# The prompt tile's scan step moved into the last stages of the make stage

## The chip, the cores and the metric

The kernel runs on one core of a Trainium2 chip. The metric is the time of one execution in device microseconds (us). TensorE (PE in the profile) does the matmuls and transposes, VectorE (DVE) and ScalarE (ACT) the element work on PSUM and SBUF, GpSimd (POOL) element work on SBUF alone, and SyncE (SP) issues most DMAs. Each engine runs its own program in order and waits on semaphores.

## The reference, cut to what matters

One layer of a diffusion backbone runs on 128 prompt tokens and 512 sample tokens: a feed-forward block, a mixer, a second feed-forward block. The mixer has two halves, attention and a gated delta rule that scans over the tokens in both directions:

```python
sol = lax.linalg.triangular_solve(a_mat, rhs, left_side=True, lower=True, unit_diagonal=True)
u0, w = sol[..., :dv], sol[..., dv:]
def step(state, inp):
    qg_n, kg_n, u0_n, w_n, qk_n, gl_n = inp
    u = u0_n - jnp.einsum('bhcd,bhde->bhce', w_n, state)
    o = jnp.einsum('bhcd,bhde->bhce', qg_n, state) + jnp.einsum('bhcs,bhse->bhce', qk_n, u)
    state = state * gl_n[..., None, None] + jnp.einsum('bhcd,bhce->bhde', kg_n, u)
    return state, o
...
y = jnp.concatenate([o_a.reshape(...), o_b_att.reshape(...)], axis=-1) @ lp['w_out']
```

The prompt starts from a zero state and its last state is an output (`new_state_delta`). The sample starts from a state that is an input (`state_delta`). So the scan of the prompt gives nothing to the scan of the sample.

## The kernel before

The 640 tokens lie in five tiles of 128 (`NT = 5`); tile 0 is the prompt. After attention the mixer goes through three parts.

**The make stage** builds, for each tile and each half of the heads, a decayed and inverted matrix (`t_all`) and a decayed product of q and k (`p_all`). There are ten units of work. Each is a sequence of 26 stages, a new unit starts every 7 stages (`MAKE_STAGES, MAKE_LAG = 26, 7`), and unit u uses the buffers and the two PSUM banks of chain u % 4. `make_schedule()` yields the pieces stage by stage, and every engine walks the same list. Units 6 and 7, the last ones of the third and fourth chain, end in stages 67 and 74; stages 75 to 88 hold only units 8 and 9, on the first and second chain. Within a unit each level of the inversion is a round trip: TensorE multiplies (L2148, L2152) or transposes (L2155), VectorE masks or subtracts the result (L1449, L1454, L1458), TensorE goes on. GpSimd masks the other operand (L1653).

**The scan** has five steps s = 0 to 4; step 0 is the prompt tile. Each step has four blocks b (two directions, two halves of the heads), each in its own PSUM bank 4 + b:

- `scan_a` (L2168; not in step 0): products of k and q with the state. VectorE makes the right side r from it (`scan_r`, L1464 and L1467: the second one reads two SBUF tensors), ScalarE scales the q part (L903).
- `scan_b` (L2184): times the inverted matrix; VectorE scales the result to u (`scan_u`, L1473).
- `scan_c` (L2194, L2198): update of the state and the output of the block; VectorE or ScalarE adds or copies them (L1483, L1495, L893).

GpSimd cuts the matrices of a step to a triangle (L1662 for `scan_b`, L1673 for `scan_c`), eight instructions a step, into `t_one` and `p_one`, which are the make buffers of the first and second chain.

**The output projection of the attention half** is cut into 16 pieces, `attention_part(0..15)`, each of 12 matmuls with 320 columns (L1683 to L1685). They are put between the stages of the scan to fill TensorE. Four pieces use one weight tile, which ScalarE rounds (`w_high`, L547) and VectorE subtracts (`w_low`, L995, two SBUF inputs); after each two pieces VectorE adds a block to x (`update_attention`, L1046). The weight slots `w_hi` and `w_lo` 0 and 1 lie on the same SBUF bytes as the make buffers of the third and fourth chain (`spare` in the profile). So before, the two first weight tiles were split after the whole make stage, beside scan step 0. Behind the scan come the normalization and gate of the scan's output (L1515, L1523, L1530 on VectorE), four transposes a tile (L2247), and then the other half of the output projection, which waits for the last of them.

In what order pieces and stages stand on TensorE is written by hand:

```python
            for s in range(NT):
                for stage in (scan_a, scan_b, scan_c):
                    if s == 0 and stage is scan_a:
                        continue
                    for b in range(4):
                        stage(s, b)
                    if (s, stage) != (0, scan_b):
                        attention_part(next(parts))
```

Before, piece 0 follows `scan_c` of step 0, pieces 1 to 12 follow the stages of steps 1 to 4, and 13 to 15 lie between the transposes.

## Time and profile before

| | us |
|---|---|
| median of 3 runs | 1739.75 |
| lowest and highest run | 1727.72, 1741.33 |
| the profiled execution | 1740.31 |
| its span in the trace | 1738.5 |
| TensorE busy in the span | 1648.7 (95%) |
| VectorE, ScalarE, GpSimd busy | 948.7, 512.9, 202.1 |
| mean granted TensorE clock | 0.97 of full speed |

The profiled execution lies 1.8 us over its own span and 0.6 us over the median. The three runs are 13.6 us apart, 0.8% of the time. TensorE is the engine that matters nearly everywhere, so the reading goes by what makes it wait and by the clock that it is granted.

### The profile page before, as it was taken

What the parts mean: (1) busy time and instruction counts of PE and PEld (TensorE: products, weight loads), DVE (VectorE), ACT (ScalarE), POOL (GpSimd) and SP (SyncE); (2) the same over time, 40 slices, a digit from 0 to 9 for tenths busy, and PEclk for the clock granted to TensorE, in tenths of its full rate; (3) what the DMA queues carried; (4) which work ended last, traced back from release to release, by engine and by line L of the source; (5) the groups of instructions that cost most, each with busy time, mean ns of one, the idle gap of its engine ahead of it and who ended that gap; (6) DMA issues with size and microseconds to landing.
All of it is one profiled execution on the core that took longest, in us unless ns stands there. A gap on an engine that the chain in (4) does not pass through costs nothing.

```text
span 1738.5 us, 27319 instructions
## 1 busy us (share of the span) xinstructions
PE 1648.7 (95%) x10807; PEld 1547.8 (89%) x10807; DVE 948.7 (55%) x1770; ACT 512.9 (30%) x978; POOL 202.1 (12%) x165
## 2 busy tenths in 40 slices
PE   6899999999999999999978999799799999999998
PEld 4899999999999999966667888799799999998886
DVE  5866666775456574447647788448652322222233
ACT  4522222221224334424441110154342222222223
POOL 0000000000000000110026666545000000000000
PEclk9999999999999999997789999899899999999999
DMA  9444444444343222210000000011212222222222
GB/s 279 124 134 142 136 144 143 137 135 141 99 144 110 56 75 64 61 49 1 1 7 1 1 1 1 1 32 37 85 37 73 72 72 75 81 61 88 71 82 88
DMA packets 183811, 136.53 MB, mean 79 GB/s; under 512 B 8192, under 2 KB 169269, under 8 KB 183605
## 3 DMA queue, kind: packets, MB, share of 16 engines
q1 hardware_dynamic: 161029, 112.91, 21.8%
q10 hardware_dynamic: 22704, 22.55, 4.3%
q8 instruction: 53, 0.87, 0.2%
q14 instruction: 25, 0.20, 0.0%
HBM read 132.03 MB, written 3.41 MB: 78 GB/s over the span
## 4 chain that ended last, share of the span: by engine, by line
PE 83%; DVE 9%; SPq 2%; issue 2%; ACT 2%; DMA 1%; POOL 0%; DVEq 0%; ACTq 0%; POOLq 0%
PE ps L1683 19%; PE ps L1685 18%; PE ps L1684 18%; PE ps L2148 3%; PE ps L1830 3%; PE ps L1828 3%; PE ps L1829 3%; PE ps L2152 3%; PE ps L2036 2%; SPq L425 2%; PE ps L1739 1%; PE ps L2184 1%; PE ps L2198 1%; PE ps L2057 1%; DMA w_raw<-in_w_ffn_in 1%
## 5 line engine op out<-in xcount | busy, mean ns | idle before, releaser
L1683 PE MATMUL ps<-h_hi,w_lo 128*128 128x320 f32 x1760 | 554.3, 315 | 12.5 <-DVE h_lo L1530 6.4
L1685 PE MATMUL ps<-h_hi,w_hi 128*128 128x320 f32 x1760 | 547.2, 311 | 0.0
L1684 PE MATMUL ps<-h_lo,w_hi 128*128 128x320 f32 x1760 | 547.0, 311 | 0.0
L995 DVE TENSOR_TENSOR w_lo<-w_raw,w_hi 128x1024 fp32r<-128x1024 f32 x158 | 195.8, 1241 | 377.4 <-ACT w_hi L547 376.2
L1683 PEld LDWEIGHTS ps<-h_hi,w_lo 128*128 128x128 f32 x1760 | 333.6, 190 | 17.0 <-DVE h_lo L1530 6.7
L1684 PEld LDWEIGHTS ps<-h_lo,w_hi 128*128 128x128 f32 x1760 | 333.5, 190 | 1.1 <-issue 0.7
L1685 PEld LDWEIGHTS ps<-h_hi,w_hi 128*128 128x128 f32 x1760 | 333.3, 189 | 0.0
L547 ACT CAST w_hi<-w_raw 128x1024 fp32r<-128x1024 f32 x158 | 165.1, 1047 | 261.6 <-PE ps L1685 111.4
L1127 DVE SCALAR_TENSOR_TENSOR ada_acc<-ada_ffn,cond,ada_acc 128x256 f32<-128x256 f32 x336 | 139.0, 480 | 1.1
L641 ACT CAST act_hi<-scratch 128x640 f32 (+1 forms) x44 | 32.0, 727 | 292.0 <-DVE scratch L1167 292.0
L1683 PE MATMUL ps<-act_hi,w_lo 128*128 128x320 f32 (+1 forms) x352 | 109.5, 311 | 0.0
L1684 PE MATMUL ps<-act_lo,w_hi 128*128 128x320 f32 (+1 forms) x352 | 108.7, 309 | 0.0
L1685 PE MATMUL ps<-act_hi,w_hi 128*128 128x320 f32 (+1 forms) x352 | 108.7, 309 | 0.0
L1828 PE MATMUL ps<-w_hi,act_lo 128*128 128x512 f32 x220 | 87.1, 396 | 1.0 <-DVE w_lo L995 1.0
L1830 PE MATMUL ps<-w_hi,act_hi 128*128 128x512 f32 x220 | 87.5, 398 | 0.0
L1829 PE MATMUL ps<-w_lo,act_hi 128*128 128x512 f32 x220 | 86.8, 394 | 0.0
L1167 DVE TENSOR_TENSOR scratch<-square,ps 128x640 f32<-128x640 f32 x44 | 36.1, 820 | 87.9 <-PE ps L1685 87.9
L634 ACT ACTIVATE square<-ps 128x640 f32<-128x640 f32 x44 | 31.0, 705 | 171.4 <-PE ps L1685 171.1
L1683 PEld LDWEIGHTS ps<-act_hi,w_lo 128*128 128x128 f32 x352 | 66.2, 188 | 0.1
L1684 PEld LDWEIGHTS ps<-act_lo,w_hi 128*128 128x128 f32 x352 | 66.2, 188 | 0.1
L1685 PEld LDWEIGHTS ps<-act_hi,w_hi 128*128 128x128 f32 x352 | 66.2, 188 | 0.0
L1618 POOL MEMSET pre<- 128x24 f32 x3 | 0.2, 122 | 547.3 <-PE ps L1685 547.3
(299 smaller groups left out, 2500.6 us busy)
## 6 DMA issues: line engine op xcount, KB each, us to landing
w_raw<-in_w_ffn_in SPq DMA_DIRECT2D x88, 512.0 KB, 3.9
w_raw<-in_w_ffn_out SPq DMA_DIRECT2D x44, 512.0 KB, 3.7
ada_ffn<-in_w_ada ACTq DMA_DIRECT2D x43, 512.0 KB, 4.2
w_raw<-in_w_in SPq DMA_DIRECT2D x28, 512.0 KB, 3.8
ada_ffn<-in_w_ada SPq DMA_DIRECT2D x13, 512.0 KB, 4.8
ada_tile<-in_w_ada SPq DMA_DIRECT2D x10, 512.0 KB, 8.6
w_raw<-in_w_out SPq DMA_DIRECT2D x8, 512.0 KB, 3.5
ada_wide<-in_w_ada SPq DMA_DIRECT2D x3, 1024.0 KB, 9.5
```

What stands on the lines that cost most here:

```text
L547: nc.scalar.copy(w_hi[s if slot is None else slot], w_raw[s][:]).then_inc(w_hi_ready, 1)
L995: nc.vector.tensor_tensor(w_lo[at], w_raw[s][:], w_hi[at].bitcast(F32), ALU.subtract)\
L1127: ins = nc.vector.scalar_tensor_tensor(a, w, col, a, op0=ALU.mult, op1=ALU.add)
L1167: nc.vector.tensor_tensor(halves(act_f[par][:]), halves(silu_g[par][:]), ps[:, 4 * par + 2:4 * par + 4, 0:HT], ALU.mult).then_inc(act_read ...
L1683: nc.tensor.matmul(out, lo, xh, start=start, stop=False)
L1684: nc.tensor.matmul(out, hi, xl, start=False, stop=False)
L1685: return nc.tensor.matmul(out, hi, xh, start=False, stop=stop)
L1828: nc.tensor.matmul(out, lo, wh, start=first, stop=False)
L1829: nc.tensor.matmul(out, hi, wl, start=False, stop=False)
L1830: ins = nc.tensor.matmul(out, hi, wh, start=False, stop=last)
L2148: four(c, lambda out, h: nc.tensor.matmul(out, m_t[c][:, h, :], t_cols[c][:, h, :], start=True, stop=True))
L2152: four(c, lambda out, h: nc.tensor.matmul(out, x_w[c][:, h, :], tt_cols[c][:, h, :], start=True, stop=True))
```

## The change

The masks, `scan_b`, `scan_u` and `scan_c` of step 0 are called from inside the walk over the make stage. `make_schedule()` yields an extra mark at the head of each stage, and at marks 69 to 81 the engines take the pieces of step 0. The masks go into the third and fourth chain's buffers (`t_first`, `p_first`), which are free from stages 68 and 75 on. ScalarE splits the first two weight tiles after step 0, and VectorE's `w_low` of the first stands now behind `scan_r` of step 1, ahead of piece 0. The pieces are dealt anew: 0 to 8 after the stages of steps 1 to 3, none after `scan_a` of step 4, 9 after its `scan_b`, and 10 to 15 behind the last `scan_c`. VectorE's `w_low` of the third and fourth weight tile moves from the middle of steps 2 and 3 to their ends; on ScalarE `w_high` goes ahead of the next step's `scan_kg` (the scaling of k, L883).

```diff
@@ constants @@
+TWO_DONE = 6 * MAKE_LAG + MAKE_STAGES
+THREE_DONE = TWO_DONE + MAKE_LAG
@@ buffers, make_schedule @@
+            t_first, p_first = [x[0] for x in spare], [x[1] for x in spare]
             for at in range((2 * NT - 1) * MAKE_LAG + MAKE_STAGES):
+                yield None, at, 0, 0, 0
@@ ScalarE @@
-            for c in range(4):
-                act.wait_ge(t_pe[c], ROUNDS[c] * PE_T)
-            for m in range(2):
-                w_high(TILE_WOUT + m, m)
...
+            for b in range(4):
+                scan_first(b)
+            for b in range(4):
+                scan_kg(1, b)
+            for m in range(2):
+                w_high(TILE_WOUT + m, m)
@@ VectorE, inside and behind the make stage @@
+                if k is None:
+                    if c == THREE_DONE + 1:
+                        scan_u(0, 0)
+                        scan_u(0, 1)
+                    if c == THREE_DONE + 2:
+                        scan_u(0, 2)
+                        scan_u(0, 3)
+                    continue
...
+            for b in range(2, 4):
+                scan_out(0, b)
+            for s in range(1, NT):
+                for b in range(4):
+                    scan_r(s, b)
+                if s == 1:
+                    w_low(TILE_WOUT, 0)
                 if s == NT - 1:
-                    update_attention(4)
                     for p in range(OUT_EARLY):
                         o_mean(p)
                 for b in range(4):
                     scan_u(s, b)
-                if s == 0:
-                    w_low(TILE_WOUT, 0)
+                if s == 1:
                     w_low(TILE_WOUT + 1, 1)
-                if s == 1:
-                    update_attention(0)
                 if s == 2:
-                    w_low(TILE_WOUT + 2, 0)
-                if s == 3:
-                    update_attention(3)
-                    w_low(TILE_WOUT + 3, 1)
+                    update_attention(1)
                 for b in range(4):
-                    if 1 <= s < NT - 1:
+                    if s < NT - 1:
                         scan_state(s, b)
-                    if s >= 1 or b >= 2:
-                        scan_out(s, b)
-                if s in (1, 2):
-                    update_attention(s)
+                    scan_out(s, b)
+                if s < NT - 1:
+                    update_attention((0, 2, 3)[s - 1])
+                if s in (2, 3):
+                    w_low(TILE_WOUT + s, s % 2)
@@ GpSimd, inside the make stage @@
+                if k is None:
+                    if c == TWO_DONE + 1:
+                        pool.wait_ge(t_dve[2], ROUNDS[2] * DVE_T)
+                    if c == THREE_DONE:
+                        pool.wait_ge(t_dve[3], ROUNDS[3] * DVE_T)
+                    if TWO_DONE < c <= TWO_DONE + 4:
+                        mask_t(0, c - TWO_DONE - 1)
+                    if THREE_DONE <= c < THREE_DONE + 4:
+                        mask_p(0, c - THREE_DONE)
+                    continue
@@ TensorE, inside the make stage and in the scan @@
+                if k is None:
+                    if c == THREE_DONE:
+                        scan_b(0, 0)
+                        scan_b(0, 1)
+                    if c == THREE_DONE + 1:
+                        scan_b(0, 2)
+                        scan_b(0, 3)
+                    if THREE_DONE + 3 <= c < THREE_DONE + 7:
+                        scan_c(0, c - THREE_DONE - 3)
+                    continue
...
-            for s in range(NT):
+            for s in range(1, NT):
                 for stage in (scan_a, scan_b, scan_c):
-                    if s == 0 and stage is scan_a:
-                        continue
                     for b in range(4):
                         stage(s, b)
-                    if (s, stage) != (0, scan_b):
+                    if (s, stage) != (NT - 1, scan_a):
                         attention_part(next(parts))
+            attention_part(next(parts))
```

Before, on TensorE, the end of the make stage and the head of step 0 (chain 0's and 1's matmuls on `m_t`, `t_cols`, `x_w`, `tt_cols`; `m_t0` to `x_w1` in the L2184 rows hold the triangle-cut matrices, `v_tok` is v, `r_s` holds u):

```order
L2152 MATMUL ps<-tt_cols1,x_w1 128x128 x4
L2155 MATMUL ps<-ident,t_all 128x128 x4
L2148 MATMUL ps<-t_cols1,m_t1 128x128 x4
L2152 MATMUL ps<-tt_cols1,x_w1 128x128 x4
L2184 MATMUL ps<-v_tok,m_t0 128x64 x4
L2184 MATMUL ps<-v_tok,m_t1 128x64 x4
L2184 MATMUL ps<-v_tok,x_w0 128x64 x4
L2184 MATMUL ps<-v_tok,x_w1 128x64 x4
L2194 MATMUL ps<-r_s0,square0 128x128 x2
L2198 MATMUL ps<-r_s0,t_cols0 128x64 x4
```

After, on TensorE, stages 76 to 80 (`spare20` and `spare30` are two of the masked matrices in the third chain's buffers, `spare01` one in the fourth chain's; L2175 is `scan_b`, L2185 and L2189 are `scan_c`, L2233, L2237 and L2240 the make stage's old L2148, L2152 and L2155):

```order
L2233 MATMUL ps<-t_cols1,m_t1 128x128 x4
L2175 MATMUL ps<-v_tok,spare20 128x64 x4
L2175 MATMUL ps<-v_tok,spare30 128x64 x4
L2240 MATMUL ps<-ident,t_all 128x128 x4
L2237 MATMUL ps<-tt_cols1,x_w1 128x128 x4
L2233 MATMUL ps<-t_cols0,m_t0 128x128 x4
L2240 MATMUL ps<-ident,t_all 128x128 x4
L2185 MATMUL ps<-r_s0,square0 128x128 x2
L2189 MATMUL ps<-r_s0,spare01 128x64 x4
L2237 MATMUL ps<-tt_cols0,x_w0 128x128 x4
```

Step 0 no longer follows the make stage but stands between the pieces of its last two units, while both are still in work.

Before, on VectorE, from the last instruction of the make stage into step 1 (`pre` is where the scan's output lies, `egc` the decay):

```order
L1454 TENSOR_TENSOR t_all<-t_all,ps 128x512
L1473 TENSOR_TENSOR r_s0<-ps,beta 128x256
L1473 TENSOR_TENSOR r_s1<-ps,beta 128x256
L1473 TENSOR_TENSOR r_s2<-ps,beta 128x256
L1473 TENSOR_TENSOR r_s3<-ps,beta 128x256
L995 TENSOR_TENSOR w_lo0<-w_raw0,w_hi0 128x1024
L995 TENSOR_TENSOR w_lo1<-w_raw1,w_hi1 128x1024
L1495 TENSOR_TENSOR pre<-pre,ps 128x256 x2
L1464 TENSOR_TENSOR r_s0<-ps,egc 128x256
```

After, on VectorE, the same place:

```order
L1502 TENSOR_TENSOR t_all<-t_all,ps 128x512
L1461 TENSOR_TENSOR pre<-pre,ps 128x256 x2
L1430 TENSOR_TENSOR r_s0<-ps,egc 128x256
L1433 TENSOR_TENSOR r_s0<-v_tok,r_s0 128x256
L1430 TENSOR_TENSOR r_s1<-ps,egc 128x256
L1433 TENSOR_TENSOR r_s1<-v_tok,r_s1 128x256
L1430 TENSOR_TENSOR r_s2<-ps,egc 128x256
L1433 TENSOR_TENSOR r_s2<-v_tok,r_s2 128x256
L1430 TENSOR_TENSOR r_s3<-ps,egc 128x256
L1433 TENSOR_TENSOR r_s3<-v_tok,r_s3 128x256
L998 TENSOR_TENSOR w_lo0<-w_raw0,w_hi0 128x1024
```

The split of the first weight tile, which piece 0 waits for, stood ahead of all of step 1 and stands now behind the eight instructions of its `scan_r`.

## Rows read from the trace of the kernel before

**Rows 1.** Windows: stretch, length, busy PE PEld DVE ACT POOL (instructions), clock, DMA

```profile
1087.30:1101.50 14.20, 12.40 (x96) 10.75 (x94) 9.32 (x15) 0.00 (x0) 5.09 (x4) 1.00 0.00 1
1101.50:1112.10 10.60, 5.95 (x40) 4.71 (x40) 4.13 (x6) 0.00 (x0) 2.52 (x2) 1.00 0.00 0
1112.10:1134.95 22.85, 20.60 (x94) 20.63 (x95) 7.46 (x9) 11.37 (x40) 21.67 (x16) 0.55 0.03 7
1134.95:1205.23 70.28, 67.79 (x565) 67.53 (x564) 43.28 (x107) 36.77 (x138) 37.51 (x32) 1.00 0.11 33
1205.23:1221.40 16.17, 9.65 (x70) 9.13 (x69) 15.58 (x29) 6.31 (x12) 0.00 (x0) 0.96 0.11 32
```

**Rows 2.** Chain of waits in the make stage's end: start, us, what

```profile
1077.59 0.89 PE ps L2148 x8
1078.48 0.44 PE ps L2144 x4
...
1088.20 0.70 DVE x_w L1449
1088.94 1.16 PE ps L2152 x8
1090.10 0.91 PE ps L2148 x8
```

**Rows 3.** Chain of waits in step 0 (to 1134) and step 1

```profile
1114.35 7.05 PE ps L2184 x32
1121.40 0.96 PE ps L2194 x4
1122.36 1.60 PE ps L2198 x8
...
1134.95 3.58 PE ps L2168 x32
...
1140.29 3.52 PE ps L2184 x32
...
1146.90 0.50 PE ps L2194 x4
1147.40 0.84 PE ps L2198 x8
```

**Rows 4.** Windows of TensorE alone where the clock was low: busy (instructions), clock, DMA

```profile
1114.35:1131.40 17.05, 17.05 (x80) 0.50 0.00 1
1131.40:1134.85 3.45, 3.45 (x15) 0.50 0.16 38
1221.40:1227.05 5.65, 5.64 (x21) 0.50 0.31 93
```

**Rows 5.** Timeline, GpSimd's masks and VectorE's two-input instructions: start, us, instruction

```profile
1122.75 4.46 POOL L1662 TENSOR_TENSOR m_t<-t_all,cst 128x512 f32<-128x512 f32 x2
1121.78 4.31 DVE L995 TENSOR_TENSOR w_lo<-w_raw,w_hi 128x1024 fp32r<-128x1024 f32 x2
...
1212.31 1.22 DVE L995 TENSOR_TENSOR w_lo<-w_raw,w_hi 128x1024 fp32r<-128x1024 f32 x1
...
1178.32 0.42 DVE L1464 TENSOR_TENSOR r_s<-ps,egc 128x256 f32<-128x256 f32 x1
...
1179.65 1.04 DVE L1467 TENSOR_TENSOR r_s<-v_tok,r_s 128x256 f32<-128x256 f32 x1
```

**Rows 6.** Timeline, the end of step 2 and step 4 (in brackets: idle time, releaser)

```profile
1170.77 1.23 DVE L995 TENSOR_TENSOR w_lo<-w_raw,w_hi 128x1024 fp32r<-128x1024 f32 x1 [8.73 <-ACT w_hi L547]
1172.99 0.38 PE L2168 MATMUL ps<-st,pre 128*128 128x128 f32 x1 [2.49 <-DVE pre L1495]
...
1198.98 1.53 DVE L1473 TENSOR_TENSOR r_s<-ps,beta 128x256 f32<-128x256 f32 x4
```

**Rows 7.** Timeline, GpSimd's first free place from stage 68 on

```profile
1071.82 1.27 POOL L1653 TENSOR_TENSOR spare<-t_all,cst 128x512 f32<-128x512 f32 x1 [1.30 <-DVE t_all L1454]
```

**Rows 8.** Timeline, TensorE behind the scan and the normalization

```profile
1221.41 0.63 PE L1683 MATMUL ps<-h_hi,w_lo 128*128 128x320 f32 x1 [6.43 <-DVE h_lo L1530]
```

More of the change, by code:

```diff
@@ new lines, in scan_u, with scan_state @@
+            def scan_u(s, b):
+                d, g, t, q = where(s, b)
+                dve.wait_ge(c_pe[b], scan_at("pe", s, b, "b"))
+                nc.vector.tensor_tensor(heads4(u_s[b][:], DK), heads4(ps[:, 4 + b, 0:256], DK),
+                                        spread(beta[:, t, q:q + 4], DK), ALU.mult).then_inc(c_dve[b], 1)
+            def scan_state(s, b):
+                d, g, t, q = where(s, b)
+                dve.wait_ge(c_pe[b], scan_at("pe", s, b, "c"))
+                dve.wait_ge(c_act[b], scan_at("act", s, b, "dec"))
+                for e in range(2):
+                    rows, cols = slice(e * DK, e * DK + DK), slice(e * DK, e * DK + DK)
+                    S = st[1][rows, d, 2 * g:2 * g + 2, cols]
+                    ins = nc.vector.tensor_tensor(S, S, heads4(ps[rows, 4 + b, 0:256], P)[:, :, cols], ALU.add)
+                ins.then_inc(c_dve[b], 1)
@@ L2116, in four, with scan_a @@
                 ins.then_inc(t_pe[c], 1)
-            for k, c, r, t, g in make_schedule():
+            def scan_a(s, b):
+                d, g = b // 2, b % 2
+                t = tile_of(s, d)
+                if s == 1:
+                    pe.wait_ge(st_in, 64)
+                    pe.wait_ge(c_act[b], scan_at("act", 0, b, "o" if b < 2 else "S"))
+                if s >= 2 or b >= 2:
+                    pe.wait_ge(c_dve[b], scan_at("dve", s - 1, b, "o"))
+                for which, at in ((4, 0), (0, 256)):
+                    for cc in range(2):
+                        ins = nc.tensor.matmul(ps[:, 4 + b, at + cc * P:at + cc * P + P],
+                                               pre[:, which + 2 * g + cc, t * P:(t + 1) * P], st[1][:, d, 2 * g + cc, :],
+                                               start=True, stop=True)
+                ins.then_inc(c_pe[b], 1)
@@ new lines, in scan_b @@
+            def scan_b(s, b):
+                if s == 0:
+                    pe.wait_ge(t_dve[2 + b // 2], ROUNDS[2 + b // 2] * DVE_T)
+                else:
+                    pe.wait_ge(c_dve[b], scan_at("dve", s, b, "r"))
+                    pe.wait_ge(c_act[b], scan_at("act", s, b, "oq"))
+                pe.wait_ge(c_pool[b], scan_at("pool", s, b, "t"))
+                r = v_tok[:, tile_of(0, b // 2), (b % 2) * 256:(b % 2) * 256 + 256] if s == 0 else r_s[b][:]
+                for h in range(4):
+                    ins = nc.tensor.matmul(ps[:, 4 + b, h * DK:(h + 1) * DK], (t_one if s else t_first)[b][:, h, :],
+                                           r[:, h * DK:(h + 1) * DK], start=True, stop=True)
+                ins.then_inc(c_pe[b], 1)
@@ new lines, in scan_c @@
+            def scan_c(s, b):
+                pe.wait_ge(c_dve[b], scan_at("dve", s, b, "u"))
+                if s < NT - 1:
+                    pe.wait_ge(c_act[b], scan_at("act", s, b, "kg"))
+                    for cc in range(2):
+                        nc.tensor.matmul(ps[:, 4 + b, cc * P:(cc + 1) * P], kg[b][:, cc * P:(cc + 1) * P],
+                                         u_s[b][:, cc * P:(cc + 1) * P], start=True, stop=True)
+                pe.wait_ge(c_pool[b], scan_at("pool", s, b, "p"))
+                for h in range(4):
+                    ins = nc.tensor.matmul(ps[:, 4 + b, 256 + h * DK:256 + (h + 1) * DK], (p_one if s else p_first)[b][:, h, :],
+                                           u_s[b][:, h * DK:(h + 1) * DK], start=True, stop=True)
+                ins.then_inc(c_pe[b], 1)
@@ L2173, in scan_b @@
-            def scan_b(s, b):
-                if s == 0:
-                    for c in (2, 3):
-                        pe.wait_ge(t_dve[c], ROUNDS[c] * DVE_T)
-                else:
-                    pe.wait_ge(c_dve[b], scan_at("dve", s, b, "r"))
-                    pe.wait_ge(c_act[b], scan_at("act", s, b, "oq"))
-                pe.wait_ge(c_pool[b], scan_at("pool", s, b, "t"))
-                r = v_tok[:, tile_of(0, b // 2), (b % 2) * 256:(b % 2) * 256 + 256] if s == 0 else r_s[b][:]
-                for h in range(4):
-                    ins = nc.tensor.matmul(ps[:, 4 + b, h * DK:(h + 1) * DK], t_one[b][:, h, :],
-                                           r[:, h * DK:(h + 1) * DK], start=True, stop=True)
-                ins.then_inc(c_pe[b], 1)
```

151 lines of the change are left out of this document (57 added, 94 removed).

## Prediction

> **What bounds the kernel now.** The first view is the page: TensorE is busy for 95% of the span, so elsewhere the change could only shift waits. It touches 1070 to 1222 us, and there the windows are the view to start from [rows 1]. The reader is to see four different limits. Up to 1101.5 us two units are in work and TensorE is nearly full; from there to 1112.1 one unit is left and TensorE works 5.95 of 10.6 us. From 1112.1 to 1134.95 (step 0 and piece 0) it is full, but at a granted clock of 0.55. In steps 1 to 4 it is full at full clock, 67.8 of 70.3 us. In the last stretch it works 9.65 of 16.2 us and VectorE 15.6: there VectorE sets the end.
>
> The chain of waits then gives the price of each piece at both clocks [rows 3]. `scan_b` of four blocks is 7.05 us at the low clock and 3.52 at the high one; `scan_c` of a block is 0.96 + 1.60 = 2.56 us low, against 0.50 + 0.84 = 1.34 high, so for four blocks 10.24 and 5.3 (the first is a little shorter). `scan_a` is 3.58 high. A piece of attention is what lies between two stages: at the low clock from 1121.40 + 10.24 = 1131.64 to 1134.95, 3.31 us, and at the high one from 1134.95 + 3.58 to 1140.29, 1.76. Work of step 0 is thus 8.8 us of high clock, and took 17.3.
>
> **The end of the make stage.** Into stages 75 to 81 come those 8.8 us of TensorE work. What hides them is the slack of two interleaved round trips: a wait for VectorE, eight slow-started matmuls and eight more, 0.70 + 1.16 + 0.91 = 2.8 us, in which TensorE could issue 0.89 + 0.89 + 0.44 = 2.2 us of work [rows 2]. So 0.6 us is free in each, and stages 75 to 81 hold four: 2.5 us hidden, 6.3 us added. The bounds are 5.7 (a fifth gap used) and 8.8 (none hidden: stage 77 has no piece of step 0 and stages 78 to 81 have one each, so gaps and pieces don't fall together everywhere). I stay near the lower, since the pieces stand at the head of stages, where the gaps are. GpSimd takes eight masks of 1.27 us more. The first fits into 1.30 us of idle time [rows 7]; the next three meet the make stage's own masks and push one that TensorE reads in the next stage by about 0.2 us. VectorE's four `scan_u` are 0.42 us each beside a TensorE that has become the later one: nothing. The sum of this term is **+6.5**. The first stages with one unit alone, 82 to 88, get nothing of step 0, though their gaps are the wider ones: that time stays as it is.
>
> **From the last matmul of the make stage (1112.1) to the end of the last `scan_c` (1205.2).** That is 93.1 us before. After, TensorE's list there is, at high clock: `scan_a` 3.6; ten pieces 17.6; `scan_b` and `scan_c` of step 1, 8.8; steps 2 and 3, 24.8; step 4, 3.6 + 3.5 + 3.5 = 10.6. That is 65.4. Two pieces fewer stand there than before (ten, not twelve). The wait of 2.3 us for the first mask of step 0 is gone, since `scan_a` of step 1 waits for nothing that is late. To this come four things.
>
> *A new wait ahead of piece 0.* It needs `w_low`, and that stands behind `scan_r` of step 1 on VectorE, which itself begins only when the make stage's last 0.70 us and two outputs of 0.42 us are done, 1.65 us after TensorE's last matmul. At the same time GpSimd starts the eight masks of step 1 in one go. A row shows what that does: two `w_low` beside masks took 4.31 us, while one alone took 1.22, and the two masks beside them took 4.46 instead of 2.5; they took turns. The second, two-input instruction of `scan_r` went from 0.42 to 1.04 us in step 3, while the one that reads PSUM stayed at 0.42 [rows 5]. Taken so here, each block of `scan_r` costs a mask and an own instruction, 1.27 + 0.42 = 1.7 us, four 6.8, and `w_low` 2.2: ready 10.7 us after the last matmul. `scan_a` ends at 3.6, so TensorE idles **7.1 us**. Without taking turns it would be 4 x 0.9 + 1.2 behind the 1.65, 6.5 us, and the wait 2.9. I take the upper value, because the masks stand back to back here as in the row.
>
> The Trainium skill, "SBUF — State Buffer", section "SBUF: two separate sides", says that VectorE's instructions with two SBUF inputs and GpSimd's hold one shared port pair by turns, whole instructions long, and the other fully blocks. By that rule the wait is the 7.1 us, without it 2.9; the 4.31 us row agrees with the rule, and it speaks against this change, which puts five such instructions where before stood two.
>
> *The clock.* Before, it fell after a wait of 2.3 us that followed the thin stretch to 1112.1, and came back only at 1134.85, after 17.05 us of step 0, which didn't lift it, and 3.45 us of 320-column matmuls, which did [rows 4]. Behind the scan it fell after 6.43 us of idle time [rows 8] and came back after 5.65 us of such matmuls. A wait of 7.1 us behind the same thin stretch will lower it again. Piece 0 is then 3.3 us of 320-column matmuls, less than the 3.45 and 5.65 us of the rows, followed by a `scan_b` of the kind that didn't lift it. So the likeliest is that it comes back with piece 1. Low are then two pieces and `scan_b`: 2 x (3.31 - 1.76) + 7.05 - 3.52 = **6.6 us**. Bounds: 1.6 (piece 0 is enough), and 13.1 (it stays low through `scan_c` and piece 2).
>
> *Step 2's stall goes.* TensorE idled 2.49 us because VectorE's `w_low` waited 8.73 us for ScalarE, which had the next step's scaling of k ahead of the cast, and the outputs stood behind it [rows 6]; some 0.4 us more came in the step after. Now the cast is ahead and `w_low` behind the outputs. What is late next is `scan_r` of step 3, behind an addition to x and `w_low`; `scan_a` and a piece, 5.3 us, cover it. The 65.4 contain no stall, so this gain of 2.9 is in the difference.
>
> *Step 4 loses its cover.* Before, u was ready from 1198.98 + 0.42 = 1199.4 [rows 6] for a `scan_c` that began 3.5 us before its end at 1205.2, so at 1201.7: 2.3 us of slack. Now 1.8 us of TensorE work ahead is gone and VectorE begins `scan_r` about 1.5 us later, behind the addition and `w_low`: 2.3 - 1.8 - 1.5 gives **+1.0** of waiting.
>
> Together 65.4 + 7.1 + 6.6 + 1.0 = 80.1, against 93.1: **-13.0**.
>
> **Behind the scan.** VectorE's list grows by one addition to x, 1.05 us, which stood in step 4, and six pieces instead of four (17.6 us of them are counted above) lie beside it: 6 x 1.76 and five transposes, 13 us on a TensorE that has 16.9. They are hidden, except some tenths. With what the earlier list loses in waits I take **+0.7**, bounds 0 and 2. The idle time before the other half of the projection shrinks from 6.4 to about 4 us. That should still lower the clock; if not, up to 2.8 us are won, half of 5.65.
>
> The sum is +6.5 - 13.0 + 0.7 = **-5.8 us**. Against the profiled execution's 1740.31 that is 1734.5, against the median of the three runs, 0.6 lower, 1734.
>
> **Rivals.** (1) *Piece 0 lifts the clock.* 3.3 us of dense matmuls is close to the 3.45 us that sufficed in one row; for this speaks that row, against it the 5.65 us of the other. The cost is 1.6 instead of 6.6: -10.9, 1729. (2) *No turns, no fall.* If GpSimd's masks and VectorE don't alternate, the wait is 2.9 us; TensorE idled 2.49 us at the end of step 2 and kept its clock. Then 4.2 and 6.6 us less: -16.6, 1723. Against it: before, 2.3 us were enough in just this place. (3) *Slower: the clock stays low through `scan_c` of step 1 and piece 2*, and the make stage hides nothing of step 0. 6.5 us more for the clock (10.24 - 5.3 and 1.55) and 2.3 for the hidden part: +3.0, 1743. It decides where the low stretch outlasts the fourth block of `scan_c`, 12.4 us of loss. For it: step 0 before, 17 us without recovery; against it: two pieces stand in the way, one more than before. (4) *The change doesn't do what it says*, if the masks come late and hold `scan_b` and with it, since TensorE is in order, the make stage: eight masks exposed are 10.2 us, +4.4, 1744. GpSimd is busy 5.1 of 14.2 us there, which speaks against it.
>
> **How the numbers follow.** The forecast gets 0.37, rival 1 0.32, rival 2 0.10, rival 3 0.14, rival 4 0.04, anything else 0.03. A measurement of this kernel tells about 1% from no change, 17.4 us; its three runs were 13.6 apart. The range reaches from rival 2 to rival 3, 1723 to 1743. Faster by over 1% is about half of rival 2 and a little of rival 1 by scatter: 0.10. Slower by over 1% takes something that I don't see: 0.02. The rest is 0.88.
>
> **What would show it.** In the windows, from the third-chain end of the make stage to its last matmul some 6 us more, with `scan_b` and `scan_c` at high clock inside it. In the chain, `scan_a` of step 1 directly behind the make stage; then TensorE idle for 3 to 7 us, released by `w_lo`, with masks and two-input instructions in alternation. The granted clock low from piece 0 to piece 1. No idle time at the end of step 2, about 1 us ahead of the last `scan_c`. Four us of idle time, not 6.4, ahead of the other half. Wrong would be most of all the length of the low stretch, since it rests on three rows; next the 7.1 us.

## The result, and the profile after

In 20 runs each, the kernel before has a median of 1737.62 us (1724.74 to 1746.52) and the changed one 1722.26 (1718.84 to 1730.46). The ratio is 0.9936, with a 95% interval from 0.9916 to 0.9956: 11.1 us less, between 7.6 and 14.6. That is within 1%, as forecast, and faster by about twice the forecast 5.8 us. The median of 1722.26 lies 0.7 us below the range; the ratio, put on the 1739.75 us from which the prediction started, gives 1728.6, inside it. Eleven of the changed kernel's 20 runs lie from 1718.84 to 1722.32 and nine from 1726.68 to 1730.46, so its median stands at the edge between two groups; the two medians alone are 15.4 us apart, and the ratio with its interval is the better measure.

The profiled execution took 1721.61 us, its span is 1719.8. It is read by stretches first, as [rows 1]: stretch, length, then busy time of PE, PEld, DVE, ACT and POOL with instructions, the granted clock, DMA share and GB/s.

```profile
1079.19:1100.20 21.01, 20.97 (x188) 20.70 (x186) 12.00 (x20) 4.10 (x16) 11.14 (x9) 1.00 0.01 2
1100.20:1112.76 12.56, 7.12 (x50) 5.89 (x51) 4.84 (x7) 4.53 (x14) 2.55 (x2) 1.00 0.09 21
1112.76:1121.74 8.98, 3.56 (x33) 3.40 (x32) 8.67 (x12) 6.02 (x24) 8.12 (x6) 0.89 0.00 0
1121.74:1131.10 9.36, 9.36 (x57) 9.36 (x57) 2.89 (x5) 0.00 (x0) 7.71 (x7) 0.74 0.18 58
1131.10:1186.36 55.26, 55.26 (x467) 55.26 (x466) 37.76 (x93) 28.38 (x107) 33.02 (x29) 1.00 0.09 30
1186.36:1203.25 16.89, 12.79 (x93) 12.53 (x92) 16.54 (x32) 7.07 (x13) 0.00 (x0) 0.95 0.10 31
```

The two-unit part of the make stage now has no idle TensorE at all, at full clock (20.97 of 21.01 us), where it had 12.40 of 14.20 [rows 1]. Its single-unit end is as thin as it was: from the same VectorE result on, the first with one unit alone (started at 1101.48 before, at 1102.14 after), it takes 10.64 us before and 10.65 after. The long low-clock stretch of 22.85 us is gone; in its place stand 8.98 us in which TensorE works 3.56, and 9.36 at a clock of 0.74. From `scan_c` of step 1 to the end of the scan TensorE never waits. Behind the scan VectorE is still the full one, 16.54 of 16.89.

The chain of waits shows the new wait (start, us, what):

```profile
1111.59 1.17 PE ps L2237 x8
1112.98 0.41 issue
1113.39 0.75 DVE pre L1461 x2
1114.14 0.34 DVE r_s L1430
1114.51 0.67 DVE r_s L1433
1115.17 0.34 DVE r_s L1430
1115.54 1.04 DVE r_s L1433
...
1118.35 1.03 DVE r_s L1433
1119.39 2.22 DVE w_lo L998
1121.74 0.60 PE ps L1714
...
1125.28 4.17 PE ps L2175 x32
```

L1461 are the two outputs of step 0, L1430 and L1433 the two instructions of `scan_r`, L998 is `w_low`, L1714 piece 0, L2175 `scan_b`. TensorE's last make matmul ends at 1112.76, `scan_a` at about 1116.3; then everything hangs on VectorE until the `w_low` is done. The engine's side is a row of TensorE's timeline (in brackets idle time and releaser), and the GpSimd masks that lie beside it are on GpSimd's:

```profile
1121.74 0.60 PE L1714 MATMUL ps<-h_hi,w_lo 128*128 128x320 f32 x1 [5.42 <-DVE w_lo L998]
...
1203.25 0.63 PE L1714 MATMUL ps<-h_hi,w_lo 128*128 128x320 f32 x1 [4.09 <-DVE h_lo L1541]
```

```profile
1113.62 2.68 POOL L1649 TENSOR_TENSOR m_t<-t_all,cst 128x512 f32<-128x512 f32 x2 [4.12 <-DVE t_all L1502]
1116.26 2.85 POOL L1649 TENSOR_TENSOR x_w<-t_all,cst 128x512 f32<-128x512 f32 x2
1119.07 3.66 POOL L1657 TENSOR_TENSOR t_cols<-p_all,cst 128x512 f32<-128x512 f32 x2
```

**Four landmarks.** To compare executions I read four points from each timeline: the start of VectorE's result of stage 74 (the ninth from the last `t_all` subtraction), the start of its last result of the make stage, the end of the last `scan_c`, and the first matmul of the projection's other half. The differences between them are the terms of the prediction; the columns are us. Up to stage 74 all kernels have the same work, but for four of GpSimd's masks of step 0, which the changed kernel puts there; they cost next to nothing: over the eleven `t_all` subtractions up to this point 33.41 us pass in the profile of the kernel before, and 33.45 to 33.47 in those of the changed kernel and its variants.

| execution | stage 74 at | A: to the last make result | B: to the end of `scan_c` | piece 0 behind the last make result | C: to the other half | rest | stage 74 to the end |
|---|---|---|---|---|---|---|---|
| before | 1084.47 | 27.65 | 93.26 | 19.28 | 16.03 | 517.09 | 654.03 |
| after | 1079.19 | 33.60 | 73.57 | 8.95 | 16.89 | 516.55 | 640.61 |
| after, second profile | 1073.09 | 34.27 | 78.24 | 10.17 | 16.89 | 517.11 | 646.51 |

Two things follow. From stage 74 on, the profiled executions differ by 13.4 or 7.5 us, and not by the 18.7 by which their spans do; the second profile (below) shows why there are two numbers. And the first column differs by up to 11 us (13 among all profiles of this study) although only those four masks in front of it were changed. The windows of TensorE alone from 825 to 925 us, in the attention part, show where that comes from; of before, after, and the second profile of the changed kernel, in this order:

```profile
825.00:925.00 100.00, 82.94 (x475) 0.81 0.01 3
```

```profile
825.00:925.00 100.00, 88.37 (x527) 0.86 0.01 3
```

```profile
825.00:925.00 100.00, 87.33 (x564) 0.93 0.02 3
```

The same part of the program got a clock of 0.81, 0.86 or 0.93 (the counts of instructions differ because the window is one of time). A share of 0.12 over 100 us is 12 us. In all eleven profiles of this study the clock in this window sorts the arrival at stage 74: 0.81 goes with 1084.5 to 1086.2 (five profiles), 0.86 with 1078.5 to 1079.3 (three), 0.93 with 1073.1 to 1073.8 (three), and each group holds kernels of different programs. So about 12 us of a single execution's time say nothing of the change. Times are therefore compared by ratios of many runs, and mechanisms by the landmarks.

### The profile page after: what moved, and what is told of

The parts are those of the page before. It is cut to its first block, busy times and chain, and to the rows that moved or that the text cites. A ratio compares the mean times of both kernels' runs of the same rounds, so it can differ in the third digit from the quotient of the medians.

```text
span 1719.8 us, 27316 instructions
## 1 busy us (share of the span) xinstructions
PE 1639.4 (95%) x10807; PEld 1539.7 (90%) x10807; DVE 949.2 (55%) x1770; ACT 511.8 (30%) x978; POOL 201.5 (12%) x165
## 4 chain that ended last, share of the span: by engine, by line
PE 83%; DVE 10%; issue 2%; ACT 2%; SPq 2%; DMA 1%; POOL 0%; DVEq 0%; ACTq 0%; POOLq 0%
PE ps L1714 18%; PE ps L1715 18%; PE ps L1716 18%; PE ps L2233 3%; PE ps L1861 3%; PE ps L1860 3%; PE ps L1859 3%; PE ps L2237 3%; PE ps L2067 2%; PE ps L1770 1%; PE ps L2175 1%; SPq L429 1%; PE ps L2189 1%; PE ps L2088 1%; PE ps L2240 1%
## 5 line engine op out<-in xcount | busy, mean ns | idle before, releaser
L1714 PE MATMUL ps<-h_hi,w_lo 128*128 128x320 f32 x1760 | 554.5, 315 | 15.7 <-DVE w_lo L998 7.5
L998 DVE TENSOR_TENSOR w_lo<-w_raw,w_hi 128x1024 fp32r<-128x1024 f32 x158 | 195.2, 1237 | 368.7 <-ACT w_hi L551 367.6
L1714 PEld LDWEIGHTS ps<-h_hi,w_lo 128*128 128x128 f32 x1760 | 333.6, 190 | 20.2 <-issue 7.4
L1714 PE MATMUL ps<-act_hi,w_lo 128*128 128x320 f32 (+1 forms) x352 | 109.6, 311 | 0.0
L1714 PEld LDWEIGHTS ps<-act_hi,w_lo 128*128 128x128 f32 x352 | 66.3, 188 | 0.1
```

Source lines behind the costliest of these rows:

```text
L998: nc.vector.tensor_tensor(w_lo[at], w_raw[s][:], w_hi[at].bitcast(F32), ALU.subtract)\
L1714: nc.tensor.matmul(out, lo, xh, start=start, stop=False)
```

## The experiments

All were timed against the kernel before: the first four together, then the next four, then the last. The kernel before had medians of 1735.54, 1735.28 and 1735.38 us beside them. The landmarks of each profile stand in one table behind the experiments.

**The changed kernel again.**

> The changed kernel as it is, as a yardstick beside the next three on the same chip. It was 0.9936 of the kernel before. In its profile the interesting place is TensorE's idle time ahead of piece 0 (5.4 us in the first profile) and the clock behind it: low for piece 0 alone, or for more. If the two groups of times seen so far (about 1720 and about 1728.5) come from this place, a profile of the upper group shows the low clock until piece 1, 5 us more; if they come from the attention part of the kernel, this place reads the same and the loss lies ahead of 1079 us.

Measured: 1722.38 us, ratio 0.9921 (0.9899 to 0.9944). This profile shows the other case of the clock. TensorE's timeline at the end of the make stage and `scan_a` of step 1, and then the windows of TensorE alone of piece 0, `scan_b`, and piece 1:

```profile
1103.54 1.16 PE L2233 MATMUL ps<-t_cols,m_t 128*128 128x128 f32 x8 [0.78 <-DVE t_cols L1506]
1105.48 1.84 PE L2237 MATMUL ps<-tt_cols,x_w 128*128 128x128 f32 x8 [0.79 <-DVE x_w L1497]
1107.11 4.73 PE L2160 MATMUL ps<-st,pre 128*128 128x128 f32 x32
```

```profile
1117.53:1121.07 3.54, 3.54 (x14) 0.50 0.51 148
1121.07:1127.79 6.72, 6.72 (x33) 0.50 0.01 2
1127.79:1130.52 2.73, 2.73 (x14) 0.66 0.00 0
```

The last eight make matmuls took 1.84 us instead of 1.16: here the clock fell within the thin stretch, ahead of any long wait. It stayed at 0.50 through piece 0 and all of `scan_b` and came back in piece 1. In the first profile of the same program it was still full up to 1112.76 and came back in `scan_b`:

```profile
1121.74:1125.28 3.54, 3.54 (x14) 0.50 0.47 148
1125.28:1129.25 3.97, 3.97 (x32) 0.84 0.02 4
```

So the forecast's case of the clock and that of rival 1 both occur, in one and the same kernel, 5.9 us apart (646.51 and 640.61). The two groups of run times, 8 us apart, can come from this or from the arrival at stage 74: every execution has both, and only the profiled ones show how much of each.

**The first w_low ahead of scan_r.**

```diff
+            w_low(TILE_WOUT, 0)
             for b in range(2, 4):
                 scan_out(0, b)
             for s in range(1, NT):
                 for b in range(4):
                     scan_r(s, b)
-                if s == 1:
-                    w_low(TILE_WOUT, 0)
```

> The first w_low stands ahead of VectorE's outputs and scan_r of step 1, not behind them. Theory (the idle time ahead of piece 0 is this w_low's place in VectorE's list): piece 0 begins where scan_a ends, the idle time of 5.4 us is gone; scan_b then meets scan_r, which ends about 2 us later than before, so it waits for blocks, in sum 1 to 2 us. If the clock does not fall, scan_b of step 1 ends some 6 us earlier than in the changed kernel: 0.9936 becomes 0.990. Rival (the clock falls anyway after the thin stretch, or the short waits inside scan_b let it fall): 5.4 us of idle time become 2 of waits, and 2 to 6 us of low clock stay or grow: a gain of 0 to 3 us.

Measured: 1714.26 us, 0.9872 (0.9844 to 0.9900), where the changed kernel beside it had 0.9921. From its timelines, the `w_low` on VectorE, and TensorE around `scan_a`, piece 0 and `scan_b`:

```profile
1119.27 1.22 DVE L998 TENSOR_TENSOR w_lo<-w_raw,w_hi 128x1024 fp32r<-128x1024 f32 x1
```

```profile
1118.46 1.95 PE L2159 MATMUL ps<-st,pre 128*128 128x128 f32 x16
1120.96 2.02 PE L2159 MATMUL ps<-st,pre 128*128 128x128 f32 x16 [0.55 <-DVE pre L1461]
1122.74 0.39 PE L1713 MATMUL ps<-h_hi,w_lo 128*128 128x320 f32 x1
...
1124.58 1.90 PE L2174 MATMUL ps<-r_s,m_t 128*128 128x64 f32 x16
1126.31 1.95 PE L2174 MATMUL ps<-r_s,x_w 128*128 128x64 f32 x16
```

The 5.42 us became 0.55 (in `scan_a`, which waits for an output of step 0 that now stands behind the `w_low`), `scan_b` met no wait at all, and the clock stayed full: `scan_b` ends 9.4 us behind the last make result, and 16.5 in the first profile of the changed kernel, 7.1 us more, where some 6 were expected. The stretch B is 66.51 us, against the 65.4 us of TensorE's own list in the prediction. The theory holds; on stretch B the price was 7.1 us against one profile and 11.7 against the other, since the wait's removal takes the clock's fall with it. Two kernels with the late `scan_c` (below), which differ in this line alone, show it again: B is 77.33 and 66.51 us.

**GpSimd's masks of step 1 later.**

```diff
             for c in range(2):
                 pool.wait_ge(t_dve[c], ROUNDS[c] * DVE_T)
+            pool.wait_ge(w_lo_ready, TILE_WOUT + 1)
             for s in range(1, NT):
```

> GpSimd begins its masks of step 1 only when the first w_low is done, so that none lies beside scan_r. Theory (VectorE's two-input instructions and GpSimd's take turns): each block of scan_r is 0.42 + 0.42 instead of 0.42 + 1.04, the w_low 1.22 instead of 2.28, and piece 0 begins about 3 us earlier than in the changed kernel, 2.5 us behind scan_a. The masks then come one in 1.27 us beside a free VectorE, the fourth 5.1 us after the w_low, and scan_b waits for them: its end is 3 to 4 us earlier than in the changed kernel. Rival (the 1.04 and 2.28 us have another cause, for instance the data): the same durations without any mask beside them, piece 0 where it was, and scan_b up to 2 us later for the masks.

Measured: 1718.80 us, 0.9892 (0.9863 to 0.9920). VectorE's timeline, `scan_r` and the `w_low` with no mask beside them:

```profile
1120.36 0.42 DVE L1433 TENSOR_TENSOR r_s<-v_tok,r_s 128x256 f32<-128x256 f32 x1
...
1122.74 0.43 DVE L1433 TENSOR_TENSOR r_s<-v_tok,r_s 128x256 f32<-128x256 f32 x1
1123.08 1.22 DVE L998 TENSOR_TENSOR w_lo<-w_raw,w_hi 128x1024 fp32r<-128x1024 f32 x1
```

All four second instructions of `scan_r` take 0.42 or 0.43 us, not 0.67 to 1.04, the `w_low` 1.22, not 2.22. Piece 0 begins 5.80 us behind the last make result, 3.15 earlier than in the changed kernel, where 3 were expected, and `scan_b` ends 3.8 us earlier, for which 3 to 4 were. One part of the expectation did not come: `scan_b` waited for none of the masks. The 1.04 us of a two-input instruction are the masks' work and nothing else. The clock still fell, in piece 0, behind an idle time of 2.27 us. The Trainium skill, "SBUF — State Buffer", section "SBUF: two separate sides", gives the rule of the shared port pair that changes hands whole instructions at a time; this pair of profiles agrees that the two hold each other up. How long a turn is comes with the idle time ahead of piece 0, below.

**scan_c of step 0 in the single-unit stages.**

```diff
-                    if THREE_DONE + 3 <= c < THREE_DONE + 7:
-                        scan_c(0, c - THREE_DONE - 3)
+                    if THREE_DONE + 7 <= c < THREE_DONE + 11:
+                        scan_c(0, c - THREE_DONE - 7)
```

> The four scan_c of step 0 stand at the head of stages 82 to 85, where one unit is left, instead of stages 78 to 81. Theory (what hides step 0 in the make stage is the wait for VectorE in each round trip, about 0.6 us, whether one unit is in work or two): four gaps of 0.66 us are filled in the single part and two of 0.6 lost in the double one, so the make stage's last matmul comes 1 to 1.5 us earlier than in the changed kernel. Rival (the single part is bound by VectorE's and TensorE's turns alone, and each scan_c stands fully in the chain): the last matmul comes 1 us later. Other side: ScalarE's casts of the output weights come later, behind scan_kg of step 1, and move piece 0 back by more than that.

Measured: 1722.78 us, 0.9929 (0.9899 to 0.9959), which can't be told from the changed kernel's 0.9921. But stretch A, the one that the edit touches, is 31.49 us, 2.11 less than 33.60. The theory's 1 to 1.5 was too little; the rival, 1 us more, is out. B is 77.33, since in this profile the clock stayed low until piece 1, as in the second profile of the changed kernel. But here it had not fallen early: `scan_a` still takes 3.74 us, as in the first profile, and the idle time ahead of piece 0 is the same.

```profile
1104.88 3.74 PE L2160 MATMUL ps<-st,pre 128*128 128x128 f32 x32
1114.04 0.60 PE L1714 MATMUL ps<-h_hi,w_lo 128*128 128x320 f32 x1 [5.42 <-DVE w_lo L998]
...
1117.37 3.51 PE L2175 MATMUL ps<-r_s,m_t 128*128 128x64 f32 x16
1120.67 3.62 PE L2175 MATMUL ps<-r_s,x_w 128*128 128x64 f32 x16
```

The two halves of `scan_b` are at the low clock, where the first profile of the changed kernel had it back (3.97 us for both). So when the clock falls does not settle when it comes back.

**Piece 0 behind scan_b.**

```diff
-                    if (s, stage) != (NT - 1, scan_a):
+                    if (s, stage) not in ((1, scan_a), (NT - 1, scan_a)):
+                        attention_part(next(parts))
+                    if (s, stage) == (1, scan_b):
                         attention_part(next(parts))
```

> The changed kernel, but piece 0 stands behind scan_b of step 1, together with piece 1, so that only the pieces and not scan_b wait for the first w_low. In the two profiles of the changed kernel the end of the last scan_c comes 73.6 and 78.2 us behind VectorE's last result of the make stage; they differ in the clock alone, which comes back in scan_b or only in piece 1. Theory (it is TensorE's long idle time that lowers the clock, and scan_b can fill it): scan_b follows scan_a block by block behind scan_r, ends near 8 us behind that last result, piece 0 begins at 9, scan_c near 12.5 at the high clock; the scan ends 67 to 68 us behind it, 6 us less than the better profile. Rival (the thin end of the make stage lowers the clock, whatever follows, until a run of 320-column matmuls lifts it): scan_b falls to the low clock, both pieces take up to 3.3 us each, scan_c begins near 16, and the gain is 0 to 3 us.

Measured: 1723.26 us, 0.9915 (0.9885 to 0.9944). In the profile B is 67.81 us, within the 67 to 68 of the theory. TensorE's timeline from the last make matmuls to piece 0:

```profile
1111.92 3.74 PE L2160 MATMUL ps<-st,pre 128*128 128x128 f32 x32
1115.49 1.90 PE L2175 MATMUL ps<-r_s,m_t 128*128 128x64 f32 x16
1117.38 1.10 PE L2175 MATMUL ps<-r_s,x_w 128*128 128x64 f32 x8
1118.78 1.10 PE L2175 MATMUL ps<-r_s,x_w 128*128 128x64 f32 x8 [0.30 <-DVE r_s L1433]
1121.08 0.38 PE L1714 MATMUL ps<-h_hi,w_lo 128*128 128x320 f32 x1 [1.20 <-DVE w_lo L998]
```

Piece 0 begins as late as in the changed kernel, 8.96 us behind the last make result, and yet nothing is lost: `scan_b` lies in what was the wait, and with waits of 0.30 and 1.20 us the granted clock was 1.00 throughout. But the measured time does not show the 6 us. Its interval, 0.9885 to 0.9944, holds both no gain and all of it. The profiled execution, 1714.54 us, is the fastest of the nine. Five others took 1723.26 to 1730.50, at a mean granted clock of 0.974 to 0.969 over the whole execution, where the profiled one had 0.978. So they lost clock that this one kept, and whether in this place is not seen.

**The stall at the end of step 2 alone,** on the kernel before.

```diff
-                if s + 1 < NT - 1:
-                    for b in range(4):
-                        scan_kg(s + 1, b)
                 if s == 2:
                     w_high(TILE_WOUT + 2, 0)
                 if s == 3:
                     w_high(TILE_WOUT + 3, 1)
+                if s + 1 < NT - 1:
+                    for b in range(4):
+                        scan_kg(s + 1, b)
...
-                if s == 2:
-                    w_low(TILE_WOUT + 2, 0)
                 if s == 3:
                     update_attention(3)
-                    w_low(TILE_WOUT + 3, 1)
...
+                if s in (2, 3):
+                    w_low(TILE_WOUT + s, s % 2)
```

> The kernel before with one part of the change alone: in steps 2 and 3 ScalarE's cast of the output weight stands ahead of the next step's scaling of k, and VectorE's w_low behind the step's outputs. Theory: the stall of 2.49 us at the end of step 2 and 0.4 us behind it go, so the stretch from the last make result to the end of the last scan_c, 93.3 us in the kernel before, becomes 90.4, and the time falls by 2.9 us. Rival (another wait, scan_r behind the addition to x and w_low, takes its place): 92 to 93.3 and no gain.

Measured: 1731.50 us, 0.9973 (0.9946 to 1.0000). B went from 93.26 to 90.24 us, 3.02 less, where 2.9 were expected; the interval of the times reaches to no change, so the gain is read from the landmarks. The waits of TensorE from 1110 to 1198 us have one entry left (engine and line, what it waited for, us in total, times, longest):

```profile
PE ps L2183 <- POOL m_t L1661: 2.3, 1, 2.3
```

That is the wait for the first mask of step 0. No other wait took the place of the stall.

**Both: early w_low and late scan_c.** The diffs are those of the two experiments.

> The first w_low ahead of VectorE's outputs and scan_c of step 0 in stages 82 to 85. Counted from the same point of the make stage (VectorE's last result of stage 74) to the end of the execution, the kernel before took 654.0 us, the changed one 640.6 and 646.5 (clock), the one with the early w_low 633.7. Theory (the two add up, since one lies behind VectorE's last result and the other ahead of it): 633.7 - 2.1 = 631.6. Rival (with scan_c so late, ScalarE's casts come too late for the early w_low, which now stands ahead of everything on VectorE, and hold the outputs, scan_a and scan_r): 633.7 or more, with idle time ahead of scan_a.

Measured: 1718.39 us, 0.9894 (0.9865 to 0.9923); 631.52 us from stage 74 to the end, where 631.6 were expected. TensorE waits 0.6 us in `scan_a` as before. Its median is above that of the early `w_low` alone, though the landmarks are 2.2 us shorter, and the intervals overlap: the timing doesn't resolve 2 us.

**And scan_b spread.**

```diff
-                    if c == THREE_DONE:
-                        scan_b(0, 0)
-                        scan_b(0, 1)
-                    if c == THREE_DONE + 1:
-                        scan_b(0, 2)
-                        scan_b(0, 3)
+                    if c in (THREE_DONE, THREE_DONE + 2, THREE_DONE + 4, THREE_DONE + 6):
+                        scan_b(0, (c - THREE_DONE) // 2)
```

with VectorE's `scan_u` one stage behind each.

> As the one before, and the four scan_b of step 0 stand one each in stages 75, 77, 79 and 81 instead of two each in 75 and 76. Theory (each round trip of the two last units has one gap of 0.6 us, and two scan_b of 1.73 us in one stage fill only one gap): two more gaps are filled, the make stage ends 1.2 us earlier, 31.5 becomes 30.3 us from the last result of stage 74 to the last of the stage, and the whole 630.4. Rival (VectorE's scan_u, spread as well, fall between its results that TensorE waits for, four times 0.35 us): no gain or up to 1.4 us longer.

Measured: 1709.75 us, 0.9865 (0.9827 to 0.9903). A is 30.66, 0.8 less (1.2 expected), the whole 630.16, the shortest of all. It is the best version of this study: 24 us of landmark time below the kernel before and 10 to 16 below the changed one. What it gains over the early `w_low`, 3.6 us, is seen in the landmarks alone; the times don't tell the two apart.

**One piece back into the scan,** on the kernel with the early `w_low`.

```diff
-                    if (s, stage) != (NT - 1, scan_a):
-                        attention_part(next(parts))
-            attention_part(next(parts))
+                    attention_part(next(parts))
...
                 if s == NT - 1:
+                    update_attention(4)
                     for p in range(OUT_EARLY):
                         o_mean(p)
...
             o_norm(1)
-            update_attention(4)
```

> The kernel with the early w_low (the second experiment), with one piece of attention given back to step 4: eleven stand ahead of the last scan_c and five behind, and the addition to x numbered 4 is back in step 4 on VectorE, ahead of the sums of squares. Theory (TensorE sets the scan, VectorE what is behind it): the scan grows by the piece, from 66.5 to 68.3 us behind VectorE's last make result; the stretch behind the scan shrinks by the addition, from 16.9 to 16.0 us, as in the kernel before; in sum 0.9 us slower, 633.7 becomes 634.6 us from the point in stage 74 to the end. Rival (scan_r and the addition in step 4 hold scan_u, and the last scan_c waits about 1 us, the term of the prediction that did not show in the changed kernel): 69 to 69.5 and 1.9 us slower. Other side (the shorter VectorE list outweighs the piece): not slower.

Measured: 1716.80 us, 0.9885 (0.9856 to 0.9914), against 0.9872. The scan grew by 1.74 us, what is behind it shrank by 1.03, and the whole is 634.57, where 634.6 were expected. Each entry is as the theory has it; none of the waits of the rival shows.

| kernel | ratio | stage 74 at | A | B | piece 0 | C | stage 74 to the end |
|---|---|---|---|---|---|---|---|
| changed, second profile | 0.9921 | 1073.09 | 34.27 | 78.24 | 10.17 | 16.89 | 646.51 |
| early `w_low` | 0.9872 | 1085.07 | 33.59 | 66.51 | 4.08 | 16.88 | 633.73 |
| masks later | 0.9892 | 1085.05 | 33.59 | 69.78 | 5.80 | 16.89 | 639.95 |
| late `scan_c` | 0.9929 | 1073.59 | 31.49 | 77.33 | 8.96 | 16.89 | 642.61 |
| piece 0 behind `scan_b` | 0.9915 | 1078.53 | 33.59 | 67.81 | 8.96 | 16.89 | 634.17 |
| stall alone, on before | 0.9973 | 1079.28 | 28.23 | 90.24 | 19.28 | 16.03 | 652.32 |
| early `w_low`, late `scan_c` | 0.9894 | 1086.18 | 31.49 | 66.51 | 4.08 | 16.89 | 631.52 |
| and `scan_b` spread | 0.9865 | 1073.84 | 30.66 | 66.52 | 4.08 | 16.88 | 630.16 |
| early `w_low`, eleven pieces | 0.9885 | 1085.13 | 33.59 | 68.25 | 4.08 | 15.85 | 634.57 |

(What is behind C varies from 515.9 to 519.7 us among all of these, in a program that is the same; the longest is that with the masks later.)

Behind the last make matmul, TensorE has one idle time of more than 2.2 us in six of the eleven profiles (the kernel before, its variant, the changed kernel twice, masks later, late `scan_c`), and none above 1.20 us in the other five. In all six the clock fell, in two of them (the changed kernel's second profile, the stall alone) already within the last make matmuls, ahead of that idle time; in the five it stayed full from there into the scan.

## Why the prediction came out as it did

| term | predicted | first profile | second profile |
|---|---|---|---|
| A: step 0 in the make stage | +6.5 | +5.95 | +6.6 |
| idle time ahead of piece 0 | 7.1 | 5.4 | 5.7 |
| low clock | 6.6 | 2.2 | 5.6 behind the start of piece 0, 1.9 ahead of it |
| wait in step 4 | 1.0 | 0 | 0 |
| B in all | -13.0 | -19.7 | -15.0 |
| C: behind the scan | +0.7 | +0.86 | +0.86 |
| sum | -5.8 | -12.9 | -7.5 |

**Term A** was right in mechanism and size. The 8.8 us of step 0 made the stretch 5.95 us longer, so 2.85 were hidden where 2.5 had been counted. All of it lies in the two-unit part. The two-unit part has nothing left to hide more (20.97 of 21.01 us); the single-unit end has, and the experiments that used it hid 5.0 us (31.49 - 27.65 = 3.84 added) and 5.8 (30.66 - 27.65 = 3.0 added). The prediction said that the wider gaps got nothing of step 0, and left it at that.

**The idle time ahead of piece 0** was the right wait in the right place for the right reason: the early `w_low` removed it, and moving the masks shortened it by 3.15 us. Its size was 1.7 us too high. The prediction charged each block of `scan_r` 1.27 + 0.42 = 1.69 us, a whole mask and a whole two-input instruction in turn. The rows show turns, but shorter ones: GpSimd's first two masks end at 1113.62 + 2.68 = 1116.30, VectorE's two-input instruction of the second block at 1115.54 + 1.04 = 1116.58, 0.28 later; two masks on, at 1116.26 + 2.85 = 1119.11, and 1118.35 + 1.03 = 1119.38, it is 0.27. A pair of turns is thus (1119.11 - 1116.30) / 2 = 1.40 us, 0.29 less than the sum of the two durations alone: in the trace the two instructions overlap by that much, and why is not shown. The first block paid only 0.67 us, and `scan_r` began 1.3 us behind TensorE's last matmul, not 1.65. The row of 1.04 us was in [rows 5] and was the better price; I took the pair of `w_low` as nearer because masks stand back to back there.

**The low clock** is the term that decided the size. The 6.6 us and rival 1's 1.6 were both on record with nearly equal chances, 0.37 and 0.32. The traces have 2.2 us in one execution and 5.6 in another: with the 8.95 and 10.17 us to the start of piece 0 taken off, what is left of B is 64.6 and 68.1, against 66.51 - 4.08 = 62.4 in the kernel with the early `w_low`. The profile with the late `scan_c`, whose clock fell as late as the first one's and came back as late as the second one's, has 77.33 - 8.96 - 62.4 = 5.9, which is the forecast's own case. In the second profile of the changed kernel the last make matmuls and `scan_a` were slow as well, another 1.9 us (0.7 in A, and 1.2 by which piece 0 begins later). So no single value was right. The prediction took the clock for a property of the program, and asked which of two values it has; it is one of the execution.

**The wait in step 4** did not come, and two things in its sum were wrong. The first is the 1.5 us by which VectorE was to begin `scan_r` later. The rows of TensorE's `scan_a` and VectorE's first `scan_r` of step 4, before and after, have it 1.09 and 1.52 us behind the start of `scan_a`, so 0.4 us later:

```profile
1191.03 3.73 PE L2168 MATMUL ps<-st,pre 128*128 128x128 f32 x32
1192.12 0.42 DVE L1464 TENSOR_TENSOR r_s<-ps,egc 128x256 f32<-128x256 f32 x1 [1.66 <-PE ps L2168]
```

```profile
1173.77 3.73 PE L2160 MATMUL ps<-st,pre 128*128 128x128 f32 x32
1175.29 0.42 DVE L1430 TENSOR_TENSOR r_s<-ps,egc 128x256 f32<-128x256 f32 x1
```

The second is the addition to x numbered 4, 1.05 us, which stood ahead of `scan_u` in step 4 before and no longer does. The prediction counted it behind the scan, in term C, and forgot that it makes u earlier; 0.43 us of that went to a wait for ScalarE's squares. VectorE's rows show u begun at 1181.48, and so ready 0.8 us before the `scan_c` that begins at 1182.67:

```profile
1179.69 1.87 DVE L1520 TENSOR_REDUCE o_sum<-t_all 128x8 f32<-128x512 f32 x3 [0.43 <-ACT t_all L944]
1181.48 1.41 DVE L1439 TENSOR_TENSOR r_s<-ps,beta 128x256 f32<-128x256 f32 x4
```

Counted from `scan_a`, 2.3 - 1.8 - 0.4 + 1.05 - 0.4 is 0.75. The forecast's wait came from the 1.5: with 0.4 in its place the sum is 0.1 us of slack even without the addition.

**Step 2's stall** was worth 3.0 us, as counted. **Term C** was right in size. The full diff also interleaves VectorE's `o_gate` and `o_low` and moves casts in this stretch, which the cut of it ahead of the prediction leaves out and for which the prediction has no term of its own; with the addition back in step 4, as in the experiment with eleven pieces, the stretch is 15.85 us against 16.03 before, so these moves are worth some 0.2 us. And the idle time ahead of the other half fell from 6.43 [rows 8] to 4.09, where 4 was named; the clock fell there all the same, as forecast.

Rival 1, -10.9 us, is what the timing is nearest to (-11.1), and its clock case is that of the first profile; but its agreement is in part luck: the forecast's idle time and its wait in step 4 were both too high, by 1.7 and 1.0 us, and stand beside a clock that is rival 1's in one profile and the forecast's in the other. Rival 2 needed masks without effect and no fall of the clock; the masks' effect is shown. Rival 3 and rival 4 did not come (the 12.4 us of loss named in rival 3 do not come out of its own rows, which give 3.1 + 3.5 + 4.9, some 11.5; nothing else rests on them): in both profiles the clock was back before `scan_c`, and the eight masks of step 0 held nothing.

Open is what decides in one execution whether the clock falls in the thin end of the make stage or not until the wait, what decides whether it comes back in `scan_b` or in piece 1, and how often each happens. The two profiles of the changed kernel show it both ways in the same code, and the one with the late `scan_c` shows that the two questions are not one.

## What to carry to other kernels

Ahead of a transfer of work into another stage, look for the instruction that the first work behind it needs and where that stands on the engine that makes it: here one `w_low` behind four `scan_r` cost 7 to 13 us from stage 74 to the end (640.61 and 646.51 against 633.73), and one moved line gave it back. Fill the gaps of the stage where one chain is left before those where two are: the former were 0.8 us a round trip and used by nothing. And compare two executions from a common point behind the last unrelated stretch, since 12 us of the spans here came from a part that no kernel had touched.

## What the runs showed of the hardware that I had not expected

In eleven profiles TensorE's stretch from 825 to 925 us, in the attention part that no kernel changed, had a mean granted clock of 0.81, 0.86 or 0.93, and of nothing between, and stage 74 came 12, 6 or 0 us later with it. The same kernel lost its clock in its last make matmuls (1.84 us for eight, not 1.16) in one execution and kept it in the next. After a wait of 5.42 us with a full clock ahead of it, 3.54 us of 320-column matmuls at the low clock were followed by a `scan_b` of 3.97 us at 0.84 in the first profile of the changed kernel; in the one with the late `scan_c`, after the same wait and the same 3.54 us, by two halves of 3.51 and 3.62 us, all of it at 0.50. And a two-input instruction of 0.42 us on VectorE beside back-to-back masks took 1.03 to 1.07 us, a pair of the two 1.40 us, and not the 1.69 of their durations alone.
